# Two transformer blocks on one core: the first product behind each norm runs all its high-half matmuls first and its low-half matmuls last

## What is computed

```python
# block 1 (w_in: 1024 x 7168)
h    = rmsnorm(x, norm_mix_g)                          # norm n1
q, k, v, xr, gr, g_attn, g_rnn = split(h @ w_in)
attn = diff_attention(q, k, v, ...)                    # 8 heads
rnn  = rg_lru_branch(xr, gr, ...)                      # convolution, gates, scan
merged = sigmoid(g_attn) * (attn @ w_proj_attn) + sigmoid(g_rnn) * (rnn @ w_proj_rnn)
x = x + merged @ w_out
h2 = rmsnorm(x, norm_mlp_g)                            # norm n2
x = x + square(relu(h2 @ w_up)) @ w_down               # 1024 -> 4096 -> 1024
# block 2
h = rmsnorm(x, mix_norm_g)                             # norm n3
...three branches (convolution, decayed attention, window attention), merged
x = x + merged @ w_mix_out
h = rmsnorm(x, xattn_norm_g)                           # norm n4
x = x + cross_attention(h, mem) @ w_xo
h = rmsnorm(x, ffn_norm_g)                             # norm n5
x = x + (silu(h @ w_gate) * (h @ w_up)) @ w_down       # 1024 -> 2816 -> 1024
out = rmsnorm(x, final_norm_g)
```

## Time and profile before

| | |
|---|---|
| three runs | 2159.88, 2167.40, 2167.91 us (median 2167.4) |
| the profiled execution | 2158.96 us, its span 2157.2 us |
| PE, PEld | busy 2037.4 us (94%), 1610.3 us (75%) |
| DVE, ACT, POOL | busy 1054.5 us (49%), 492.2 us (23%), 1220.5 us (57%) |
| granted clock, mean of the span | 0.966 of 2.4 GHz |
| HBM read | 173.75 MB, 82 GB/s over the span |

### The profile page before, as it was taken

How to read it: one execution, slowest core, us unless ns; L and a number is a source line. 1 busy time by engine, 2 the same in 40 slices (tenths; PEclk the granted TensorE clock), 3 DMA queues, 4 the chain that set the end, 5 groups by cost and what they waited for, 6 DMA issues and landing times.

```text
span 2157.2 us, 23419 instructions
## 1 busy us (share of the span) xinstructions
PE 2037.4 (94%) x9015; PEld 1610.3 (75%) x9015; DVE 1054.5 (49%) x1507; ACT 492.2 (23%) x985; POOL 1220.5 (57%) x1003
## 2 busy tenths in 40 slices
PE   6999979999999999998999988999998899999997
PEld 4666658887878888886677766777777878888886
DVE  7656658995373223158454554333464564213134
ACT  4444433332121101021233222000131221001012
POOL 5233227787767666665233333666676756667662
PEclk8999979999999999999899888999999999999999
DMA  5122103333333333333112211333333323333321
GB/s 154 51 59 59 57 22 92 97 99 89 98 93 93 98 95 93 97 98 88 30 49 59 69 45 44 88 88 88 107 107 89 108 69 98 95 91 98 98 83 54
DMA packets 341169, 177.39 MB, mean 82 GB/s; under 512 B 14453, under 2 KB 338203, under 8 KB 341060
## 3 DMA queue, kind: packets, MB, share of 16 engines
q1 hardware_dynamic: 339044, 173.28, 27.9%
q10 hardware_dynamic: 2016, 2.62, 0.6%
HBM read 173.75 MB, written 2.13 MB: 82 GB/s over the span
## 4 chain that ended last, share of the span: by engine, by line
PE 82%; DVE 13%; issue 3%; ACT 2%; DMA 0%; ACTq 0%; DVEq 0%; SPq 0%
PE bank L599 23%; PE bank L601 23%; PE bank L603 23%; PE bank L717 4%; PE bank L694 2%; PE bank L683 1%; PE bank L665 1%; DVE HS L1643 1%; DVE IT L1632 1%; DVE ACC L1637 1%; DVE XC L1613 1%; DVE HS L1642 1%; PE bank L896 1%; PE bank L897 1%; PE bank L898 1%
## 5 line engine op out<-in xcount | busy, mean ns | idle before, releaser
L572 POOL TENSOR_TENSOR WL<-RAW,WH 128x1024 fp32r<-128x1024 f32 (+3 forms) x331 | 810.7, 2449 | 27.6
L599 PE MATMUL bank<-HH,WH 128*128 128x512 f32 x1560 | 631.0, 404 | 3.7 <-DVE HL L1413 3.7
L603 PE MATMUL bank<-HH,WL 128*128 128x512 f32 x1560 | 624.9, 401 | 0.0
L601 PE MATMUL bank<-HL,WH 128*128 128x512 f32 x1560 | 621.9, 399 | 0.0
L568 POOL TENSOR_TENSOR gate<-gate 128x1 f32<-128x1 f32 x331 | 79.6, 240 | 877.9 <-PE bank L603 811.9
L599 PEld LDWEIGHTS bank<-HH,WH 128*128 128x128 f32 x1560 | 297.9, 191 | 77.0 <-issue 10.6
L603 PEld LDWEIGHTS bank<-HH,WL 128*128 128x128 f32 x1560 | 297.7, 191 | 67.2 <-issue 7.1
L601 PEld LDWEIGHTS bank<-HL,WH 128*128 128x128 f32 x1560 | 298.0, 191 | 64.7 <-issue 5.3
L569 POOL TENSOR_SCALAR WH<-RAW 128x1024 fp32r<-128x1024 f32 (+3 forms) x331 | 342.9, 1036 | 1.4 <-issue 0.2
L1683 DVE TENSOR_TENSOR X<-X,bank 128x512 f32<-128x512 f32 x80 | 54.9, 687 | 210.4 <-PE bank L603 210.3
L1413 DVE SCALAR_TENSOR_TENSOR HL<-X,PARAM,HH 128x512 fp32r<-128x512 f32 x40 | 89.2, 2230 | 30.6 <-ACT HH L1031 30.6
(11 more groups left out here) (389 smaller groups left out, 3192.5 us busy)
## 6 DMA issues: line engine op xcount, KB each, us to landing
RAW<-in_w_in SPq DMA_DIRECT2D x107, 512.0 KB, 3.8
RAW<-in_w_up SPq DMA_DIRECT2D x32, 512.0 KB, 4.1
RAW<-in_w_down SPq DMA_DIRECT2D x32, 512.0 KB, 4.1
RAW<-in_w_ffn_gate SPq DMA_DIRECT2D x22, 512.0 KB, 3.8
RAW<-in_w_ffn_up SPq DMA_DIRECT2D x22, 512.0 KB, 3.8
RAW<-in_w_xkv SPq DMA_DIRECT2D x16, 512.0 KB, 3.9
RAW<-in_w_ffn_down SPq DMA_DIRECT2D x16, 512.0 KB, 3.6
RAW<-in_w_proj_attn SPq DMA_DIRECT2D x8, 512.0 KB, 3.9
```

What stands on the lines that cost most here:

```text
L572: nc.gpsimd.tensor_tensor(WL[:, s, 0:k, :], RAW[:, s, 0:k, :], WH[:, s, 0:k, :].bitcast(F32), ALU.subtract).then_inc(S_[f"unit_cut{s}"], 1)
L599: mm(psum[s][:, 0:n], WH[:, s, k, :], hi(k), start=(k == 0), stop=False)
L601: mm(psum[s][:, 0:n], WH[:, s, k, :], lo(k), start=False, stop=False)
L603: last = mm(psum[s][:, 0:n], WL[:, s, k, :], hi(k), start=False, stop=(k == tiles - 1))
```

## The change

A product with `ready` now runs in three passes over k: WH times the high half for all k, WL times the high half for all k, WH times the low half for all k. The wait for tile k's high half stands before its matmul in the first pass, the wait for its low half before its matmul in the third. The number of matmuls, the bank, the weights and the other products stay.

```diff
+                if ready:
+                    high_ready, low_ready = ready
+                    for k in range(tiles):
+                        high_ready(k)
+                        mm(psum[s][:, 0:n], WH[:, s, k, :], hi(k), start=(k == 0), stop=False)
+                        yield
+                    for k in range(tiles):
+                        mm(psum[s][:, 0:n], WL[:, s, k, :], hi(k), start=False, stop=False)
+                        yield
+                    for k in range(tiles):
+                        low_ready(k)
+                        last = mm(psum[s][:, 0:n], WH[:, s, k, :], lo(k), start=False, stop=(k == tiles - 1))
+                        if k == tiles - 1:
+                            last.then_inc(S_[f"product{s}"], 1)
+                        yield
+                    return
                 for k in range(tiles):
-                    if ready:
-                        ready(k)
                     mm(psum[s][:, 0:n], WH[:, s, k, :], hi(k), start=(k == 0), stop=False)
...
             def cut_of(tag):
-                def ready(k):
-                    pe.wait_ge(*norm_event(tag, "hh", k + 1))
-                    pe.wait_ge(*norm_event(tag, "hl", k + 1))
-                return ready
+                return (lambda k: pe.wait_ge(*norm_event(tag, "hh", k + 1)),
+                        lambda k: pe.wait_ge(*norm_event(tag, "hl", k + 1)))
```

More of the change, by code:

```diff
@@ L821, in cut_pair @@
             def cut_pair(hi, lo, base=0):
[L822 to L825, removed]
+                return (lambda k: pe.wait_ge(S_[hi], base + k + 1),
+                        lambda k: pe.wait_ge(S_[lo], base + k + 1))
             for i in range(2):
```

## The result

| | before | changed |
|---|---|---|
| 15 runs each, median | 2167.43 us | 2175.69 us |
| lowest, highest | 2156.24, 2171.46 | 2168.72, 2181.72 |
| ratio, 95% interval | | 1.0048 (1.0033 to 1.0063) |
| span of the profiled execution | 2157.2 us | 2167.4 us |

The changed kernel is slower, by 0.33 to 0.63%. The forecast was 2179.9 us, 16.3 us more than before. Measured are 10.2 us more between the two spans and about 10.4 by the ratio, right at the 0.5% that was named as the line to "no change". The two medians differ by 8.3 us; the 15 runs of each kernel lie in two groups, 5 of them in the lower one, whose medians (2159.3 and 2169.2) are 9.9 us apart.

What follows compares the result with a forecast made beforehand. PE's stream of matmuls was taken as the bound. Later product ends, 12.9 us, and the clock, 3.4, gave 16.3 us more (13 to 18), from 2163.6 to 2179.9 us, range 2169 to 2188.

Steps and rivals of the forecast that it cites:

- What bounds the kernel: PE's stream of matmuls, 82% of the span, is the bound; a place counts by when its product's last matmul starts.
- The wait for HL: All of PE's waits for HL, 3.7 us and mostly at n1, were the most the change could take away.
- The formula for a product: Where PE waited for tile 7's low half, the product ends later by 3.27 us less the low half's lag behind the high.
- part 1: Places where tile 7's low half came last, from 0.64 us per first feed-forward group to 2.49 at n1; 11.66 us more.
- The clock: Holes in PE's work at n1 and out2 drop the granted clock to half, 1.7 us each, 3.4 together.
- n1 on the path: At n1 the product ends 2.49 us later, and DVE's lateness behind it reaches PE whole.
- one of the signs that the prediction named against itself: The prediction is wrong if L607 waits, the step differs from 0.2335 us, or later ends vanish by the next product.
- parts 1 and 2: Places where PE waited for the low half, 11.66 us, and places where it did not wait, 1.20; together 12.9.
- the rival with a part swallowed: Clock unmoved and n1's 2.5 us swallowed while DVE is busy: 10.4 us more, 2174.0 us; chance 0.24.
- The gain beyond 3.27 us: Rival: low halves over 3.27 us late at ten places outside n1 and out2, each gaining 0.5: 2158.6 us; chance 0.04.
- The long fall of the clock: Rival: the clock stays low twice as long at n1 and out2, 19.7 us more or above, 2184 to 2187; chance 0.18.
- The level: Known times lay in two pairs, 2159.0 and 2159.9, 2167.4 and 2167.9; the forecast started from their mean, 2163.6 us.

Runs made afterwards that it cites:

- n1_only: Three passes at the first product behind norm n1 alone, all else as in the kernel before; ratio 1.0026 (1.0007 to 1.0046).
- warm_before: The kernel before with 44 spare matmuls in the idle stretch ahead of head 0; median 2157.32 us, ratio 0.9972 (0.9953 to 0.9992).
- warm_after: The changed kernel with 32 spare matmuls in the idle stretch ahead of head 0; median 2166.86 us.
- low_last: The kernel before, each tile of all 15 products doing its two high-half matmuls first, then waiting for the low half; one time, 2162.09 us.
- out2_filled: The kernel before with three passes at out2's first product alone and 14 spare matmuls ahead of tile 7's high-half wait; one time, 2163.39 us.

## Why the prediction was right or wrong

**What bounds the kernel**: right. PE's stream sets the end, and each place but n1 counted by the end of its product. The wait for HL was not all that the change could take away, there were 1.4 us for MGCL and 0.6 for FFL beside it; nothing hung on that.

**The formula for a product**: right to 0.12 us at the 13 places where the clock did not change, and at three more points that the experiments added: the hole filled at out2 (2.40 against 2.48), the distance beyond break-even (-0.52 against -0.55, or -0.47 by its limit), and the order with two matmuls moved. The values of part 1 are a little high throughout (0.64 against 0.57, 1.13 against 1.06), mainly because PE starts sooner behind a high half than the 0.14 us taken from a low one: in the first group from UH ACT ends the high half at 684.21 and PE starts at 684.26. The step behind the wait is longer than 0.2335 on both sides (0.31 before, 0.34 changed), which cancels.

**The clock**: the mechanism was right and shown at out2, where filling the hole keeps the clock at 1.00 and saves 1.5 us (1.7 were taken). At n1 it is there as well, 4.34 in place of 2.49 us, but as a clock that comes up 11 us later and not as one that falls. No run filled the holes there; that it is the clock rests on the steps of the eight L603 matmuls, which cost 1.55 of the 1.85 us. By other traces this excess would be smaller: n1_only's product takes 14.99 us.

**n1 on the path**: wrong. "DVE's lateness reaches PE whole" is the step that failed. It rested on DVE's idle 1.35 us and on PE's wait of 11.1 us for DVE. Both were true, but a chain on DVE isn't of a fixed length when it runs beside POOL's cuts: of 4.64 us, 1.23 arrived. It was one of the signs that the prediction named against itself, a later end that vanishes on the way. With 1.2 in the place of n1's 4.2 the sum is 13.3.

**The remainder**: 13.3 less what parts 1 and 2 and out2's clock were set too high is 12.3, and 10.2 arrived. About 2 us were lost on the way, nearly half of it in block 2's branches. There the granted clock changes several times and at other moments in each trace: around 1030 us it is low for 23.9 us before and for 20.5 in the changed kernel, and the delay shrinks from 4.7 to 3.0 us over this stretch. From there to 1341 us it goes up and down with the clock, and 3.8 are left. The low stretches from n3 to out2 add up to 68.3 us before and 64.9 in the changed kernel. In the traces of warm_before and warm_after they add up to 68.3 in both, and 5.0 us are left there. So this part goes with the moments of the clock, though no run tested it; the pieces of 0.2 to 0.5 us elsewhere stay open.

**The rivals**: the result lies between the forecast and the rival with a part swallowed. That rival's figure, 10.4 us more, was close, but its reason was not: it had the clock unmoved and n1 gone, while in the traces the clock moved at both places. The gain beyond 3.27 us exists, but the kernel has no place in that range (and by part 1 that rival had eight places outside n1 and out2 to count with, less than the ten that it took). The long fall of the clock did come, but at head 0, in executions of either kernel, and no part of the change.

**The level**: placing the forecast on the mean of two levels was sound, and the reason for the levels is now known in the main: head 0's clock. The forecast of 0.70 for "slower by over 0.5%" was too sure, with 1.0048 measured; the error is n1's term, and 2 us of the remainder. The cost itself, 16.3 us with 13 to 18 as its range, missed the measured 10.2; the measured 2175.69 us lies within 2169 to 2188 because that range was wide enough for both levels, not because the sum was right.

## What to carry to other kernels

Ahead of a wait put as much work as is free of it. Splitting a wait in an early and a late one helps only if the work moved behind the early one is less than the late one saves: here 14 matmuls of 0.2335 us moved against a low half 0.8 to 2.6 us late. Taking 2 matmuls out from behind the wait for the low half, as low_last does, made nine products shorter and none longer by more than 0.01 us. Before costing a gap on TensorE, look whether the clock falls behind it, and before carrying a delay along an engine's chain, look which of its operations are stretched by a neighbour, since a shift changes that.

## What the runs showed of the hardware

- After an idle stretch ahead of head 0 (3.4 to 11.2 us in the traces) the granted clock (0.50, 1.2 GHz) came back by 63 us in five of the traced kernels without spare matmuls there and only at 86 to 89 us in six others, with the same work on PE, though PE was shown busy without a gap there (23.00 of 23.00 us from 62 to 85 in all six). The length of the idle stretch doesn't sort them: the clock was up by 55.9 us behind 5.4 us of it and low until 85.9 behind 3.4. With PE kept busy through the stretch the clock stayed up in both traces, and the 11 runs of each of the two kernels lay in one group. Why a busy PE isn't given the clock back for 25 us the runs don't show.
- A DVE operation on 128x8 elements took 0.17 us alone and up to 2.25 us beside POOL's cut of 128x1024; 24 of them cost 13.5 us or 9.2 us by their position against POOL. One on 128x512 elements took 0.75 or 2.74 us.
- The step between matmuls on 512 columns with alternating or repeated halves is the same: 5.60 us for 24 in low_last is 0.2333 each, and within the three passes of out2_filled a pass of 8 took 1.86 us (1553.58 to 1555.44).
